# A hybrid decoder layer with 32 experts: the expert biases are loaded ahead of the store of the spread bias line

## The reference, cut to what matters

```python
sh_m, sc_m, g_m, sh_f, sc_f, g_f = split(silu(c) @ w_ada + b_ada, 6)     # the modulation
h = rms_norm(x, norm_mix) * (1 + sc_m) + sh_m
q, k, v, u = split(h @ w_in)              # 8 heads of 64, 2 key heads; u goes to the pooling mixer
q, k = rms_norm(q, q_norm), rms_norm(k, k_norm)
s = q @ k.T / 8 + rel_table[t5_bucket(rel)]     # window of 128, blocks of 128, and a sink
attn = softmax([s, sink]) @ v
x = x + g_m * ([attn, pool] @ w_out)
h = rms_norm(x, norm_ffn) * (1 + sc_f) + sh_f
topv, topi = top_k(h @ w_router + b_router, 4)           # 32 experts, 4 for each token
for each expert e, for the tokens that chose it:
    gate, up = split(h[tok] @ w1[e] + b1[e])
    act = (clip(up, -7, 7) + 1) * min(gate, 7) * sigmoid(1.702 * min(gate, 7))
    y += softmax(topv) * (act @ w2[e] + b2[e])
out = x + g_f * y
```

## Time and profile before

| | |
|---|---|
| median of three runs | 1314.0 us |
| profiled execution | 1314.37 us |
| its span | 1312.6 us |
| TensorE busy | 1209.7 us (92%) |
| VectorE, ScalarE, GpSimd busy | 687.4, 489.4, 324.8 us |
| mean granted clock of TensorE | 0.961 |
| moved by DMA | 474.12 MB, mean 361 GB/s |

### The profile page before, as it was taken

How to read it: one execution, slowest core, us unless ns; L and a number is a source line. 1 busy time by engine, 2 the same in 40 slices (tenths; PEclk the granted TensorE clock), 3 DMA queues, 4 the chain that set the end, 5 groups by cost and what they waited for, 6 DMA issues and landing times.

```text
span 1312.6 us, 17500 instructions
## 1 busy us (share of the span) xinstructions
PE 1209.7 (92%) x6428; PEld 723.2 (55%) x6428; DVE 687.4 (52%) x1085; ACT 489.4 (37%) x703; POOL 324.8 (25%) x352
## 2 busy tenths in 40 slices
PE   5999999979999979998899989998979998999985
PEld 3554555633675645764675347655447656465642
DVE  2162633653795775453694245537535527576731
ACT  5031522312564533333473133324323324454530
POOL 2323420221212314113322411134412125131221
PEclk8999999969999989999899999999979999999996
DMA  9950966299999999999999999999999999999996
GB/s 338 323 165 11 418 257 254 104 374 396 395 386 374 404 410 389 407 389 369 401 414 406 406 397 401 417 363 402 410 396 406 397 351 410 411 411 411 409 412 254
DMA packets 95145, 474.12 MB, mean 361 GB/s; under 512 B 17058, under 2 KB 19449, under 8 KB 46993
## 3 DMA queue, kind: packets, MB, share of 16 engines
q1 hardware_dynamic: 76154, 444.76, 84.1%
q0 software_dynamic: 18240, 26.57, 8.1%
q10 hardware_dynamic: 664, 1.65, 0.4%
HBM read 459.46 MB, written 32.53 MB: 375 GB/s over the span
## 4 chain that ended last, share of the span: by engine, by line
PE 56%; DMA 13%; DVE 6%; issue 2%; ACT 1%; POOL 1%; SPq 1%; POOLq 0%; DVEq 0%; ACTq 0%
PE bank L2544 53%; DMA raw<-in_w 5%; DMA yd<-gu,idx_s 2%; DVE rawr L2360 2%; DMA out_y_prompt<-gu,slot_tok 2%; PE bank L2592 2%; DMA g_last<-modd 1%; DMA yd<-ost,idx_s 1%; PE bank L2568 1%; POOL gu L2043 1%; ACT hi L2171 1%; DVE ost L2394 1%; DVE gu L2324 0%; DVE gu L2322 0%; DVE gu L2331 0%
## 5 line engine op out<-in xcount | busy, mean ns | idle before, releaser
L2360 DVE TENSOR_TENSOR rawr<-raw,hi 128x1024 fp32r<-128x1024 f32 x288 | 351.6, 1263 | 105.4 <-ACT hi L2171 103.5
L2171 ACT CAST hi<-raw 128x1024 fp32r<-128x1024 f32 x288 | 294.7, 1047 | 164.2 <-PE bank L2544 138.0
L2544 PE MATMUL bank<-raw,xT_even 128*64 128x512 f32 (+1 forms) x704 | 136.9, 605 | 0.0
L2029 POOL DMA_INDIRECT yd<-ost,idx_s x31 | 56.6, 1825 | 322.1 <-ACT ost L2154 321.2
L2544 PE MATMUL bank<-raw,aT 128*32 128x256 f32 (+1 forms) x992 | 112.9, 474 | 11.3 <-DMA raw<-in_w 11.3
L2544 PE MATMUL bank<-hi,xTh_odd 128*128 128x512 f32 x224 | 76.7, 424 | 18.4 <-DVE rawr L2360 18.2
L2544 PE MATMUL bank<-hi,xTh_even 128*128 128x512 f32 x256 | 85.1, 414 | 5.1 <-DVE rawr L2360 5.1
L2544 PE MATMUL bank<-hi,aTh 128*128 128x512 f32 x240 | 78.1, 407 | 10.9 <-DVE rawr L2360 10.9
L2544 PE MATMUL bank<-raw,xT_odd 128*32 128x512 f32 (+1 forms) x544 | 78.5, 601 | 7.6 <-DMA raw<-in_w 7.6
L2322 DVE TENSOR_SCALAR gu<-bank 128x512 f32<-128x512 f32 (+1 forms) x50 | 31.4, 628 | 99.8 <-PE bank L2544 99.8
L2134 ACT ACTIVATE gu<-gu 128x512 f32<-128x512 f32 (+1 forms) x50 | 29.2, 583 | 142.0 <-DVE gu L2322 142.0
(11 more groups left out here) (397 smaller groups left out, 1803.6 us busy)
## 6 DMA issues: line engine op xcount, KB each, us to landing
raw<-in_w SPq DMA_DIRECT2D x355, 1024.0 KB, 12.6
raw<-in_w SPq DMA_DIRECT2D x50, 512.0 KB, 12.0
raw<-in_w_ada SPq DMA_DIRECT2D x21, 1024.0 KB, 8.9
w_in_sb<-in_w_in SPq DMA_DIRECT2D x4, 1280.0 KB, 15.1
w_out_sb<-in_w_out SPq DMA_DIRECT2D x4, 1024.0 KB, 10.2
early<-in_w SPq DMA_DIRECT2D x4, 1024.0 KB, 13.5
ada_more<-in_w_ada SPq DMA_DIRECT2D x3, 1024.0 KB, 16.6
xs<-in_x_prompt SPq DMA_DIRECT2D x4, 512.0 KB, 11.5
```

The lines of the kernel that those rows point to most:

```text
L2029: gp.indirect_dma_start(yd_of[n], bass.IndirectOffsetOnAxis(ap=m.idx_s[:, p % 6, b:b + 1], axis=0), out_rows(p, b), None, bounds_check=lim ...
L2171: nc.scalar.copy(m.hi[:, (2 * n + h) % HI, :], m.raw[:, slot, h * D:(h + 1) * D]).then_inc(hi_done, 1)
L2360: v.tensor_tensor(m.rawr[slot][:, half], m.raw[:, slot, half], m.hi[:, (2 * n + h) % HI, :].bitcast(F32), ALU.subtract).then_inc(lo_done, 1)
L2544: return nc.tensor.matmul(out, lhsT, rhs, start=start, stop=stop, skip_group_check=True)
```

## The change

GpSimd issues the two loads of `bb` before it waits for `line_ready` and stores `skew`, and no longer after the wait for `mr_ready`. That wait now stands between the store and the small loads.

```diff
             for n in range(4):
                 gp.wait_ge(win_in[n], 16)
+            gp.dma_start(m.bb[:, 0:2 * D], i["b1"][0]).then_inc(s.bb_in, 16)
+            gp.dma_start(m.bb[:, 2 * D:3 * D], i["b2"][0]).then_inc(s.bb_in, 16)
             gp.wait_ge(s.line_ready, 1)
             gp.dma_start(m.skew.rearrange("h (a b n) -> (h a) b n", a=P // NH, b=NH, n=LINE),
                          m.line[:].unsqueeze(1).to_broadcast([P, NH, LINE])).then_inc(s.skew_out, 16)
             gp.wait_ge(s.mr_ready, WHOLE // 2)
-            gp.dma_start(m.bb[:, 0:2 * D], i["b1"][0]).then_inc(s.bb_in, 16)
-            gp.dma_start(m.bb[:, 2 * D:3 * D], i["b2"][0]).then_inc(s.bb_in, 16)
             for dst, src in ((m.sinks_bc[:], i["sinks"].to_broadcast([P, NH])),
```

## The result

The changed kernel took 1308.4 us (median of 7 runs, 1304.4 to 1311.8) where the kernel before took 1315.2 (7 runs): a ratio of 0.9937, 95% interval 0.9918 to 0.9955. A second comparison gave 1307.1 against 1314.6, 0.9946 (0.9928 to 0.9964). (A ratio is worked out from all runs, so it can lie about 0.1% from the quotient of the two medians.) The time lies in the forecast range, but the gain is 7 us, not 3.2. At 0.63% and 0.54% it lies just outside the 0.5% within which I had put it with a chance of 0.89, though both intervals reach back over that mark.

What follows compares the result with a forecast made beforehand. TensorE's stall before tile 0's query transposition, set by bb's landing, was taken as the bound; removing it gives 2.77 to 3.26 us, taken as 3.2, so 1314.0 becomes 1310.8 us, range 1307.2 to 1315.0.

Steps and rivals of the forecast that it cites:

- the forecast range: Whole kernel: the range meant to hold 8 in 10, 1307.2 to 1315.0 us, around a forecast of 1310.8.
- What bounds the kernel: TensorE's stall at 72 to 75 us: bb's landing, through bb_hi, bb_lo, hss and kd, sets its restart at 74.92.
- Steps 1 and 2: GpSimd's loads of bb leave 2.77 us earlier and ahead of the skew store, so they land sooner than about 64.4.
- the 2.77 us of earlier issue: bb's loads on GpSimd: issued 2.77 us earlier, worth at least a gain of 2.77 us even with a late landing.
- my 52 to 54: Landing of bb, in us, with the store no longer ahead of it and the DMA engines idle as it leaves.
- my 62.8 to 66.2: Landing of the skew store, in us, instead of 61.8, with bb's 384 KB ahead of it.
- Step 3: TensorE's transposition of tile 0's queries (L1509) starts at 71.66, not 74.92: a gain of 3.26 us, all of the stall.
- Steps 4 to 6: Behind the stall: no new wait at tile 1, later skew store costs nothing, small loads about 1 us earlier, off the path.
- "116.8": TensorE: z and u end at 116.8 us in place of 120.
- "the same clock in the kernel's favour": TensorE behind the routing: 6 to 8 us less at the low clock level, giving 1307 us; chance 0.10.
- a drop of clock could cost some of the gain: TensorE behind the routing: 10 us more at the low clock level, giving 1315.8 us; chance 0.10.
- the median would show only part of such a shift: TensorE's clock behind the routing: shifts occur in the earlier runs as well (1313.31 to 1317.89), so the median shows only part.

Runs made afterwards that it cites:

- late_split: Kernel before with GpSimd's list unchanged; bb_hi on ScalarE and bb_lo on VectorE moved behind the four prompt tiles; ratio 0.9929.
- bb_lo_late: Changed kernel with three extra maxima of bb with itself on VectorE ahead of bb_lo, about 9 us; ratio 1.0003.
- order_only: Against the kernel before: bb's loads moved ahead of the skew store but still waiting for the modulation (mr_ready); ratio 0.9945.
- wait_only: Against the kernel before: bb's loads freed of the wait for the modulation (mr_ready) but still behind the skew store; ratio 0.9991.
- before_2: Kernel before run again without edit, for a second profile; ratio 1.0006.
- before_3: Kernel before without edit, third profile, taken last; no time or ratio given, stall 7.63 us.
- before: The kernel without the change; median 1315.2 us in the first comparison, 1314.6 in the second; first profiled execution 1314.37 us.
- after: First profile of the changed kernel, no further edit; profiled execution 1306.01 us, median 1308.4 us, ratio 0.9937.
- after_2: Changed kernel run again without edit, for a second profile; 1307.1 us, ratio 0.9946.
- before_pe_late2: Kernel before with 7 extra multiplications on TensorE ahead of tile 1's z, 6.0 us in all; 1313.8 us, ratio 1.0005.

## Why the prediction was right in its mechanism and wrong in its size

- *What bounds the kernel.* Right: the landing of bb, through bb_hi, bb_lo and hss, set TensorE's restart. late_split and bb_lo_late show it from both sides, one by taking the stall away without an earlier landing, the other by keeping it with one.
- *Steps 1 and 2, landing.* Right in the reason: behind the store. order_only and wait_only show it. They also show that the 2.77 us of earlier issue, which I had taken as the lower bound of the gain, are worth nothing by themselves: where bb left without that wait (before_2 at 48.74, before_3 at 49.28, wait_only at 49.41) it landed at 64.7, 66.4 and 66.3, and in the first profile of before at 65.0. The landing came later than my 52 to 54 in after (56.4) and within them in after_2 (52.8): I had read from one profile that the DMA engines are nearly idle as bb leaves, and in after, where SyncE's modulation loads had left before it, they were 0.95 busy. That of skew came at 65.8, within my 62.8 to 66.2.
- *Step 3, the sum.* This is the term that failed: "The gain is 74.92 - 71.66 = 3.26 us, all of the stall". The stall was 3.10 us in the one execution that I had, and 6.13 and 7.63 in the next two. I took its length as a property of the kernel. Its end is nearly one (74.6 to 76.4 in three profiles, with the landing of bb); its start moves with TensorE's progress up to 36 us. That profile happened to have the low clock there for most of the stage, the case in which the stall is shortest. The three stalls average 5.6 us. For an execution that arrives as late as that one the term was right: after_2 starts its last L1516 at 70.05 (69.93 in the earlier trace rows), and has L1509 at 71.78 where I forecast 71.66, and the end of u at 116.9 where I forecast 116.8.
- *A second part of it was missing:* in the executions with the stalls of 6.13 and 7.63 us TensorE's clock went down, and the transposition behind them took 1.12 us in place of 0.66. From L1509 to the start of u it is 17.57 us in the first profile of before (92.49 - 74.92) and 19.68 and 19.65 in the other two: another 2.1 us. With it the loss is 7.2 us on average, where the sum has 3.26. The earlier trace rows show a clock of 1.00 in the short stall, so nothing in that profile told of it.
- *Steps 4 to 6.* Right: no new wait before 120, SyncE's next load at 123.74 with TensorE's lead, and the later skew cost nothing. "116.8" for the end of u came true in after_2 and was 3.3 us too late for after (113.55), which arrived earlier.
- *The rivals.* The one with "the same clock in the kernel's favour" (0.10) named the cause nearest to what happened, but put it behind the routing, not ahead of the stall. I held that a drop of clock could cost some of the gain; in the kernel before it was the stall that swallowed what a full clock had gained. The Trainium skill (TensorE: Matmul & The Clock Gate, the part on the gate) says that the gate's phase isn't tied to the kernel's start. The traces agree: one kernel shows 0.52, 1.00 and 0.76 from 29 to 36 us. I concluded from it that the median would show only part of such a shift. Ahead of the stall it is otherwise: a lead of TensorE is lost in the kernel before and kept in the changed one, so it is part of the difference between the medians.
- *What was luck.* That 1308.4 lies in my range (1307.2 to 1315.0) is owed to the lower end, which I had set for a clock in the kernel's favour behind the routing. That isn't what happened; the forecast itself was 1310.8, a gain less than half of the measured one.
- *The rest of the way.* The lead of after's profile over before's was 6.51 us at the start of u and 8.4 at the end. TensorE waited 2.13 us for a load of w_ada at 145, in place of 0.86, and the low clock behind the routing ended sooner. Stages of after, to be held against the earlier trace rows:

```profile
270.00:275.00 5.00, 4.70 (x28) 4.46 (x29) 4.44 (x11) 0.12 (x1) 2.59 (x2) 0.63 1.01 420
275.00:280.00 5.00, 4.92 (x24) 1.63 (x24) 4.63 (x7) 0.46 (x1) 0.38 (x3) 1.00 1.04 388
```

There the clock is back before 275, with the kernel before just after 285. Whether the change has a part in that isn't settled: this stretch lasted 17 to 20 us in the three profiles of before and 14 us in all the others, but bb_lo_late and wait_only are among those others and have no gain, and the way from u to the end took no longer in before than in the kernels without the stall (above), which speaks against a part of any size.

## What to carry to other kernels

A stall in one profile has two ends; ask what sets each. If one is a transfer's landing and the other the progress of an engine whose clock differs between executions, its length in one execution says little: take two or three profiles, or hold the engine back by a known amount and see what the time does. And look at what stands ahead in the same DMA queue before you count a removed wait: here two loads, 384 KB together, needed to be ahead of a store of 1532 KB, not earlier.

## What the runs showed of the hardware

- Loads of 256 and 128 KB issued from GpSimd took 12.8 to 16.6 us behind a store of 1532 KB that had been issued 0.8 to 2.8 us before them (before, before_2, before_3, wait_only, late_split), and 3.3 to 8.8 us ahead of it (6.8 to 8.8 where SyncE's 2 x 1024 KB had left before them, 3.3 to 4.0 where they hadn't). In before_pe_late2, 8.5 us behind the store, they took 8.0 and 10.3.
- Stalls of TensorE of 4.68 to 7.84 us were followed by transpositions at 1.2 GHz in all five profiles that have one (1.11 and 1.12 us for the first one, against 0.60 to 0.66); the one of 3.10 us wasn't.
- An added 6.0 us of TensorE was worth 0 us in one kernel and 6.1 in the other, which differ by the place of two DMA issues.
